# Attention scores alternate row halves of the array, edge masks in PSUM, exponentials pair by pair

## What is computed

```python
# 8 q heads / 2 kv heads, head_dim 64, window 128, SEQ = 256, float32
scores = einsum('bnqkgd,bnskd->bnkgqs', qb, kb) * (HEAD_DIM ** -0.5)
valid = (abs(qpos - kpos) <= WINDOW) & (kpos >= 0) & (kpos < s)
scores = where(valid, scores, NEG_INF)
m = maximum(max(scores, axis=-1), sink_b)          # one learned sink logit per head
p = exp(scores - m)
denom = sum(p, axis=-1) + exp(sink_b - m)
out = einsum('bnkgqs,bnskd->bnqkgd', p / denom, vb)
# ... per-group RMSNorm, concat with the short-conv heads, @ w_out, residual add
x = x + (swiglu(h) if layer == 0 else moe_swiglu(h))
```

## Time and profile before

| what | us |
|---|---|
| median of 3 runs | 1282.02 |
| lowest and highest run | 1281.47, 1283.46 |
| span of the profiled execution | 1280.5 |
| PE busy in it | 1247.6 (97%) |
| PE weight loads | 970.4 |
| DVE busy | 580.6 |
| ACT busy | 434.4 |
| bytes moved by DMA | 419.46 MB, 328 GB/s mean |

### The profile page before, as it was taken

How to read it: one execution, slowest core, us unless ns; L and a number is a source line. 1 busy time by engine, 2 the same in 40 slices (tenths; PEclk the granted TensorE clock), 3 DMA queues, 4 the chain that set the end, 5 groups by cost and what they waited for, 6 DMA issues and landing times.

```text
span 1280.5 us, 31578 instructions
## 1 busy us (share of the span) xinstructions
PE 1247.6 (97%) x14347; PEld 970.4 (76%) x14347; DVE 580.6 (45%) x931; ACT 434.4 (34%) x674; POOL 10.8 (1%) x35
## 2 busy tenths in 40 slices
PE   7999999999998999999999999999999999999997
PEld 6787788888787776777777777766677778768894
DVE  5696555456496655564766737521100002210103
ACT  6565444446562544543644535300000000000002
POOL 3000000000000000000000000000000000000000
PEclk9999999999998999999999999999999999999999
DMA  9335644273102999999999999999999999999993
GB/s 345 134 132 198 257 177 174 113 263 136 62 1 95 422 420 421 421 425 421 419 422 420 424 422 420 420 421 421 421 418 416 397 395 400 411 418 419 423 421 156
DMA packets 109015, 419.46 MB, mean 328 GB/s; under 512 B 4632, under 2 KB 8768, under 8 KB 100688
## 3 DMA queue, kind: packets, MB, share of 16 engines
q1 hardware_dynamic: 107776, 416.30, 80.3%
q0 software_dynamic: 544, 1.12, 0.3%
q10 hardware_dynamic: 560, 0.01, 0.0%
HBM read 416.37 MB, written 1.05 MB: 326 GB/s over the span
## 4 chain that ended last, share of the span: by engine, by line
PE 83%; DMA 7%; DVE 5%; ACT 3%; issue 1%; SPq 0%; DVEq 0%
PE bank L2223 27%; PE bank L2287 14%; PE bank L1840 12%; PE bank L1841 12%; PE bank L1842 12%; DMA ring<-in_moe_w_down 5%; DMA ring<-in_moe_w_up 2%; PE bank L2152 2%; PE bank L2158 2%; ACT raw_d L865 1%; DVE lo L1190 1%; DVE mx L1280 1%; DMA raw_gu<-in_w_in 1%; DVE raw_d L1277 1%; ACT w_hi L799 1%; PE bank L1919 1%
## 5 line engine op out<-in xcount | busy, mean ns | idle before, releaser
L1632 DVE TENSOR_TENSOR w_lo<-ring,w_hi 128x896 fp32r<-128x896 f32 (+2 forms) x192 | 202.1, 1088 | 79.9 <-ACT w_hi L799 73.8
L2223 PE MATMUL bank<-ring,late_acts 128*32 128x224 f32 x4736 | 234.0, 353 | 0.0
L2223 PEld LDWEIGHTS bank<-ring,late_acts 128*32 128x32 f32 x4736 | 188.9, 110 | 40.9 <-issue 5.0
L799 ACT ACTIVATE w_hi<-ring 128x896 fp32r<-128x896 f32 (+2 forms) x192 | 176.2, 948 | 117.6 <-PE bank L1842 76.2
L1060 ACT ACTIVATE silu_buf<-bank 128x224 f32<-128x224 f32 (+2 forms) x76 | 29.1, 394 | 433.8 <-PE bank L2223 433.8
L1840 PE MATMUL bank<-hi,act_hi 128*128 128x512 f32 (+1 forms) x400 | 155.3, 388 | 5.4 <-DVE gated L1449 2.4
L1842 PE MATMUL bank<-hi,act_lo 128*128 128x512 f32 (+1 forms) x400 | 153.0, 382 | 0.0
L1841 PE MATMUL bank<-lo,act_hi 128*128 128x512 f32 (+1 forms) x400 | 152.9, 382 | 0.0
L1190 DVE TENSOR_TENSOR lo<-raw_gu,hi 128x1024 fp32r<-128x1024 f32 x96 | 113.9, 1222 | 48.6 <-ACT hi L799 48.4
L1655 DVE TENSOR_TENSOR silu_buf<-silu_buf,bank 128x224 f32<-128x224 f32 (+2 forms) x76 | 32.0, 434 | 207.3 <-PE bank L2223 186.0
L799 ACT ACTIVATE hi<-raw_gu 128x1024 fp32r<-128x1024 f32 x96 | 97.7, 1059 | 40.3 <-PE bank L1842 36.3
(11 more groups left out here) (249 smaller groups left out, 1349.0 us busy)
## 6 DMA issues: line engine op xcount, KB each, us to landing
ring<-in_moe_w_up SPq DMA_DIRECT2D x59, 1792.0 KB, 20.7
ring<-in_moe_w_gate SPq DMA_DIRECT2D x58, 1792.0 KB, 20.0
ring<-in_moe_w_down SPq DMA_DIRECT2D x53, 1792.0 KB, 20.6
ring_after<-in_moe_w_down SPq DMA_DIRECT2D x11, 1792.0 KB, 19.7
raw_gu<-in_w_in SPq DMA_DIRECT2D x7, 2048.0 KB, 12.5
raw_gu<-in_dense_w_gate SPq DMA_DIRECT2D x5, 2048.0 KB, 7.9
raw_gu<-in_dense_w_up SPq DMA_DIRECT2D x5, 2048.0 KB, 12.4
raw_d<-in_dense_w_down SPq DMA_DIRECT2D x5, 2048.0 KB, 14.4
```

The source lines that it names most:

```text
L799: return nc.scalar.activation(out, in_, ACT.Copy, **kw)
L1632: v.tensor_tensor(w_lo[:, n % WP, 0:b - a], flat(u)[:, a:b], w_hi[:, n % WP, 0:b - a], ALU.subtract).then_inc(w_lo_done, 1)
L2223: ins = mm(bank[b][32 * c:32 * c + 32, 0:n], acts[STEPS[s][0]][:, k, g.col:g.col + 32], w[:, c], start=k == 0, stop=k == KT - 1)
```

## The change

It does these things, in both layers and both query tiles:

- `scores` issues heads in the order 0, 4, 1, 5, 2, 6, 3, 7 where it was 0 to 7, so that successive matmuls use different halves of the array's rows. Banks are complete in the order 0, 2, 1, 3 (`SCORE_BANKS`), with one signal each as before.
- `masked_scores` no longer writes scaled and masked scores to SBUF. It adds the mask in place in PSUM, only on the 128-key block in which a key can be out of the window (128x256 over a pair of heads), reduces the PSUM bank to two maxima, and makes `nmx` for the pair with one small operation from a negated sink; `masked_done` is signalled for each pair. The sink's difference comes once at the end with a signal of its own.
- `exps` waits for each pair, reads scores from PSUM, and scales within the activation.
- `turn_probs` goes by pairs in the same order.
- DVE does `probT_copy(layer, 0)` directly after pieces 16 and 17, ahead of z and the denominators.
- One operation in layer 0's `rope` negates the sink logits (`nsink`, 128x16).

```diff
+        SCORE_BANKS = (0, 2, 1, 3)
             def exps(layer, t):
-                act.wait_ge(masked_done, 2 * layer + t + 1)
-                for h in range(NH):
-                    nc.scalar.activation(prob[:, h * 256:(h + 1) * 256], prob[:, h * 256:(h + 1) * 256], ACT.Exp,
-                                         bias=nmx[:, t, h:h + 1], accum_out=psums[:, t, h:h + 1]).then_inc(exp_done, 1)
+                for n, b in enumerate(SCORE_BANKS):
+                    act.wait_ge(masked_done, 4 * (2 * layer + t) + n + 1)
+                    for i in range(2):
+                        h = 2 * b + i
+                        nc.scalar.activation(prob[:, h * 256:(h + 1) * 256], bank[b][:, i * SEQ:(i + 1) * SEQ], ACT.Exp,
+                                             bias=nmx[:, t, h:h + 1], scale=HD ** -0.5,
+                                             accum_out=psums[:, t, h:h + 1]).then_inc(exp_done, 1)
+                act.wait_ge(sinkd_done, 2 * layer + t + 1)
                 nc.scalar.activation(esink[:, t, :], sinkd[:, t, :], ACT.Exp).then_inc(exp_done, 1)
...
+                    link(v.tensor_scalar(nsink[:, :, :], sink_sb[:, :, :], -1.0, None, ALU.mult))
...
             def masked_scores(layer, t):
                 i = 2 * layer + t
-                for b in range(4):
-                    dve.wait_ge(scores_done, 4 * i + b + 1)
-                    two_heads = prob[:, b * 512:(b + 1) * 512].rearrange("p (h n) -> p h n", h=2)
-                    link(v.scalar_tensor_tensor(
-                        out=two_heads, in0=bank[b][:, :].rearrange("p (h n) -> p h n", h=2), scalar=HD ** -0.5,
-                        in1=mask[:, t, :].unsqueeze(1).to_broadcast([P, 2, SEQ]), op0=ALU.mult, op1=ALU.add))
-                    ins = v.tensor_reduce(mx[:, 2 * b:2 * b + 2], two_heads, AX, ALU.max)
-                link(ins)
-                link(v.tensor_tensor(mx[:, :], mx[:, :], sink_sb[:, layer, :], ALU.max))
-                v.tensor_scalar(nmx[:, t, :], mx[:, :], -1.0, None, ALU.mult)
-                v.tensor_tensor(sinkd[:, t, :], sink_sb[:, layer, :], mx[:, :], ALU.subtract).then_inc(masked_done, 1)
+                edge = slice(P, SEQ) if t == 0 else slice(0, P)
+                for n, b in enumerate(SCORE_BANKS):
+                    dve.wait_ge(scores_done, 4 * i + n + 1)
+                    two = slice(2 * b, 2 * b + 2)
+                    two_heads = bank[b][:, :].rearrange("p (h n) -> p h n", h=2)
+                    link(v.tensor_tensor(two_heads[:, :, edge], two_heads[:, :, edge],
+                                         mask[:, t, edge].unsqueeze(1).to_broadcast([P, 2, P]), ALU.add))
+                    link(v.tensor_reduce(mx[:, two], two_heads, AX, ALU.max))
+                    v.scalar_tensor_tensor(out=nmx[:, t, two], in0=mx[:, two], scalar=-HD ** -0.5,
+                                           in1=nsink[:, layer, two], op0=ALU.mult, op1=ALU.min).then_inc(masked_done, 1)
+                dve.wait_ge(masked_done, 4 * (i + 1))
+                v.tensor_tensor(sinkd[:, t, :], sink_sb[:, layer, :], nmx[:, t, :], ALU.add).then_inc(sinkd_done, 1)
...
                 pieces(16, 18)
+                probT_copy(layer, 0)
...
                 denominators(layer, 0)
-                probT_copy(layer, 0)
                 pieces(18, 22)
...
             def scores(layer, t):
-                for b in range(4):
-                    for i in range(2):
-                        h = 2 * b + i
-                        rows = slice(HD * (h // 4), HD * (h // 4) + HD)
-                        ins = mm(bank[b][:, i * SEQ:(i + 1) * SEQ], qT[rows, h % 4, t * P:(t + 1) * P],
+                for c in range(4):
+                    for g in range(NKV):
+                        b, i = 2 * g + c // 2, c % 2
+                        rows = slice(HD * g, HD * g + HD)
+                        ins = mm(bank[b][:, i * SEQ:(i + 1) * SEQ], qT[rows, c, t * P:(t + 1) * P],
                                  kT[rows, :], start=True, stop=True)
-                    ins.then_inc(scores_done, 1)
+                        if i == 1:
+                            ins.then_inc(scores_done, 1)
             def turn_probs(layer, t):
-                for h in range(NH):
-                    pe.wait_ge(exp_done, (NH + 1) * (2 * layer + t) + h + 1)
-                    for kt in range(NT):
-                        c = (h % 2) * 256 + kt * P
-                        ins = tr(bank[h // 2][:, c:c + P], prob[:, h * 256 + kt * P:h * 256 + kt * P + P], ident[:, :])
+                for n, b in enumerate(SCORE_BANKS):
+                    pe.wait_ge(exp_done, (NH + 1) * (2 * layer + t) + 2 * n + 2)
+                    for h in (2 * b, 2 * b + 1):
+                        for kt in range(NT):
+                            c = (h % 2) * 256 + kt * P
+                            ins = tr(bank[b][:, c:c + P], prob[:, h * 256 + kt * P:h * 256 + kt * P + P], ident[:, :])
                 ins.then_inc(probT_done, 1)
```

More of the change, by code:

```diff
@@ L387, in build_trunk @@
         nmx = sb("nmx", [P, NT, NH])
+        nsink = sb("nsink", [P, 2, NH])
         sinkd = sb("sinkd", [P, NT, NH])
@@ L548, in build_trunk @@
         qkT_done, qT_out, kT_out = sem("qkT_done"), sem("qT_out"), sem("kT_out")
-        scores_done, masked_done, exp_done, rden_done = sem("scores_done"), sem("masked_done"), sem("exp_done"), sem("rden_done")
+        scores_done, masked_done, sinkd_done, exp_done, rden_done = (
+            sem("scores_done"), sem("masked_done"), sem("sinkd_done"), sem("exp_done"), sem("rden_done"))
         probT_done, probT_out_a, probT_out_v = sem("probT_done"), sem("probT_out_a"), sem("probT_out_v")
```

## The result

| kernel | median us | lowest and highest | span of the profiled execution |
|---|---|---|---|
| before | 1281.74 (4 runs) | 1281.13, 1283.46 | 1280.5 |
| after | 1296.19 (4 runs) | 1294.88, 1298.31 | 1295.1 |

The ratio of after to before is 1.0111, 95% interval 1.0100 to 1.0123. The change makes the kernel 14.4 us slower, where 7.5 us faster was forecast; the time lies far above the range.

A forecast was written before the change was run, and what follows sets the result against it. PE was taken to bound the kernel, with attention waits in the mixers. Terms 0.86 + 1.05 + 0.46 + 0.86 + 0.50 = 3.73 us a mixer, 7.5 in both, gave 1274.5 from 1282.02; range 1272.6 to 1278.2.

The forecast's parts named there:

- What bounds the kernel now: Opening section: PE holds 83% of the chain; three attention waits lose 1.05, 0.46 and 0.85 us; experts' stream keeps its length.
- a slower side: Rival in scores: the halves take turns instead of overlapping, each call some 1.5 us worse, total 1284.0; chance 0.03.
- values(1): Second attention call: the 0.85 us wait goes, but PE then waits for DVE's copy, so the gain is 0.50.
- Alternating: In scores: heads issued in turns from both row halves save 0.86 us a call, 1.72 a mixer, all on PE's path.
- The 0.11: In scores: us allowed for the second half's start; without it alternating would gain 0.97 a call.
- the order rule: In scores: matmuls start and end strictly in program order, last start after 1.87 us, not 1.73; total 1275.1, inside the forecast's range.
- turn_probs(0): First exponential transposes: took 2.82 us where about 1.77 suffices; pairs end the wait for ACT and gain 1.05.
- Masks in PSUM: In DVE's masking: an in-place addition of 128x256 costs 0.42 us, a pair 1.26; dearer-PSUM rival 1275.5 to 1278.3, chance 0.06 above 0.69.
- the upper bound of 0.69: In DVE's masking: us for the PSUM addition at most, from the masked write of 128x512; second call then loses 0.5.
- scores(1): Second scores call: its 0.46 us wait for DVE's copy of probabilities goes because the copy moves ahead of z.
- the 1.8 us that I allowed for it: After routing: extra cost if all 6.9 us of the lower clock level fall over PE's dense work.
- something I do not see: Remaining case with no place or size given; chance 0.01.

The follow-up runs named there:

- the change without the shift: The changed kernel with nsink declared after the last SBUF tile, so every other tile keeps its address from before the change: 1273.85 us, ratio 0.9937.

## Why the prediction was wrong

**The step that failed** is the last paragraph of "What bounds the kernel now": the experts' stream starts earlier and "its length is left as it is". It grew by 21.9 us, and that is the whole of the miss: 1296.19 less 21.9 is 1274.3, against 1274.5 forecast. I had gone through the instructions that the change adds and moves, and its one new tile only as the output of an instruction (0.16 us, correctly nothing). What a declaration does to the addresses of all tiles behind it stood nowhere, neither as a term nor as a rival. Among the rivals there was a slower side, but it was another one, and it did not come.

The trace of the kernel before had the warning. The chain gave PE 83% and I took the experts for PE's stage; the window of 500 to 900 us, shown above, was not among the rows of the prediction. A DMA share of 1.02 for 400 us at a stretch says that transfers have nothing in reserve: whatever makes them longer makes the kernel longer. Had I asked which rows would change if the loads were 3% dearer, the answer would have been 20 us and more, three times the gain under discussion. "It is wrong if the experts' stretch grows" was in my list, and that is what showed.

**The terms of the sum**, by the change without the shift (30.23 and 34.13 us for a mixer), against 3.73 predicted and 3.90 measured. Between the starts on PE it is 2.59 to the second `scores`, 0.93 from there to `turn_probs(1)` and 0.38 from there to `values(1)`, where the working had 2.37, 0.86 and 0.50. So the near hit for the mixers holds a term that was too large and several that were too small:

- Alternating: 0.97 a call, not 0.86. Growing windows over L1908 (columns as in the earlier trace rows) show two records begun by 47.56 and none more to 47.85, then two at a time:

```profile
47.50:47.56 0.06, 0.01 (x2) 1.00 0.00 0
47.50:47.85 0.35, 0.30 (x2) 1.00 0.00 0
47.50:47.88 0.38, 0.33 (x4) 1.00 0.00 0
47.50:48.10 0.60, 0.55 (x6) 1.00 0.00 0
47.50:49.18 1.68, 1.63 (x16) 1.00 0.05 10
```

  The 0.11 that I allowed for the second half's start is not there; the gain is the upper bound. Both halves' first records begin together, though the first half's second record stands between them in the program, so the order rule, taken record by record, fails here as it did on the row of before. Taken by whole matmuls of two records each, it is not broken by these rows; the row of before breaks it either way. What was wrong is that each 0.86 was called PE's own: by itself it is worth nothing, as alternating alone shows.
- `turn_probs(0)`: 1.91 us long with no wait, as said. The next product starts 1.67 after it, where the working had 1.77, so the gain is 1.15 and not 1.05.
- Masks in PSUM: an addition takes 0.43 where I took 0.42. Timeline of DVE after, the first pair, and the copy for which `values(1)` waits:

```profile
48.71 0.43 DVE L1287 TENSOR_TENSOR bank<-bank,mask 128x256 f32<-128x256 f32 x1 [2.02 <-PE bank L1908]
49.18 0.69 DVE L1289 TENSOR_REDUCE mx<-bank 128x2 f32<-128x512 f32 x1
49.91 0.16 DVE L1290 SCALAR_TENSOR_TENSOR nmx<-mx,nsink 128x2 f32<-128x2 f32 x1
49.98 0.43 DVE L1287 TENSOR_TENSOR bank<-bank,mask 128x256 f32<-128x256 f32 x1
...
76.34 1.29 DVE L1303 COPY raw_d<-bank 128x512 f32<-128x512 f32 x2 [0.22 <-PE bank L1920]
```

  From one pair to the next it is 49.98 - 48.71 = 1.27, predicted 1.26. So the upper bound of 0.69 for the row that was missing was not needed. ACT's exponentials, timeline of ACT after, first and last of the tile:

```profile
50.10 0.47 ACT L870 ACTIVATE raw_d<-bank,nmx 128x256 f32<-128x256 f32 x1 [3.56 <-DVE nmx L1290]
...
54.36 0.47 ACT L870 ACTIVATE raw_d<-bank,nmx 128x256 f32<-128x256 f32 x1
```

  Less the 0.54 by which this mixer began later, they run from 49.6 to 54.3, predicted 49.5 and 54.3. Read from PSUM one takes 0.47 where it took 0.49 from SBUF, so that costing this at nothing was right.
- `scores(1)`: the 0.46 was gained, but booked to the move of the copy. Without the move it is gained just the same.
- `values(1)`: the new wait for DVE's copy is there with 0.51; DVE stood idle 0.22 before the copy, where the working had 0.6 (75.5 against 76.1). PE goes on 3.39 after the start of the transposes. The working had 3.27, though its own terms, 1.92 + 0.03 + 1.28, add up to 3.23.
- The low clock after routing lasts 10.2 us where it was 6.9 before. Windows over it (columns as there), first of the changed kernel, then of the change shifted by 256 B:

```profile
398.20:408.40 10.20, 7.39 (x25) 7.30 (x26) 6.89 (x34) 2.44 (x6) 0.00 (x0) 0.50 0.69 236
```

```profile
397.20:407.40 10.20, 6.74 (x23) 6.65 (x24) 6.85 (x39) 3.09 (x6) 0.00 (x0) 0.50 0.69 235
```

  In the second, the experts' stretch is 1273.1 - 400.5 = 872.6, no longer than before (872.4), and no longer than with `nsink` at the end (873.2), where the low stretch lasts 6.8 us. So the length of the low stretch did not show in the time, and the 1.8 us that I allowed for it was not needed.

**The chances** had 0.93 on faster, 0.03 on slower and 0.01 on "something I do not see". They were chances among cases of the instruction streams only.

## What to carry to other kernels

A new tile is an edit to every address behind it. In a kernel whose long stage is bound by transfers, look at where the destination of the loads begins before and after, against a multiple of 256 B, and either declare small tiles last or pad them; both gave back the whole loss here. A DMA share at 1.0 with packets of one constant duration is a state that an edit elsewhere can break, and the spread of the packet durations is the quickest way to see that it did.

And a chain of several engines has to be shortened at the step that ends last: against the kernel before, alternating alone gave nothing, the rest of the change without alternating 4.0 us (1278.55), and both together 8.5.

## What the runs showed of the hardware that was not expected

- Loads into SBUF at 32, 64, 128 or 192 B past a multiple of 256 cost 3.4 to 5.5 ns a packet more, on 3584 B (140 ns) and on 14336 B (535 ns) alike, and a stream that fills the DMA engines falls from 421 to between 409 and 412 GB/s. The four kernels are not equally slow (1307.3, 1304.9, 1301.3 and 1303.6 us, each on another chip), and why is open.
- Matmuls on the two halves of the array's rows, issued in turns, begin within 0.01 us of each other and run at each half's full pace: 16 fp32 records of 64x256 last 2.00 us in place of 2.96.
- An addition in place in a PSUM bank costs DVE what a copy out of it does, 0.43 against 0.42 us for 128x256, and a reduction of 128x512 takes 0.69 from PSUM as from SBUF.
